# Half of a conditioning matrix-vector product taken off TensorE and given to GpSimd, in a two-block transformer kernel

## The reference, cut to what matters

```python
mod = jax.nn.silu(c) @ ada_w[l] + ada_b[l]            # [1, 1024] @ [1024, 6144]
sh_m, sc_m, g_m, sh_f, sc_f, g_f = jnp.split(mod, 6, axis=-1)
hn = adaln(x, mix_norm_g[l], sh_m, sc_m)              # rmsnorm(x) * g * (1 + scale) + shift
...                                                   # projections, four attentions, w_out
x = x + g_m[:, None, :] * y
hn = adaln(x, ffn_norm_g[l], sh_f, sc_f)
...                                                   # SwiGLU (layer 0) or 8 experts (layer 1)
x = x + g_f[:, None, :] * f
```

## Time and profile before

| | |
|---|---|
| median of 3 runs | 2811.58 us (2811.15 to 2815.84) |
| the profiled execution | 2816.96 us, of which the span of its instructions is 2815.1 us |
| TensorE busy | 2707.3 us, 96% of the span |
| VectorE busy | 1712.9 us, 61% |
| ScalarE busy | 1319.6 us, 47% |
| GpSimd busy | 27.1 us, 1% |
| HBM read | 625.06 MB, 222 GB/s over the span |
| granted TensorE clock | 0.984 of 2.4 GHz over the span |

### The profile page before, as it was taken

The page is one execution under the profiler, slowest core; times in us unless marked ns, Lnnn a source line. Parts: engine busy times, 40 slices in busy tenths (PEclk is TensorE's granted clock), DMA queues, the critical chain, the costliest instruction groups (busy, mean ns, idle before and its releaser), DMA issues.

```text
span 2815.1 us, 39528 instructions
## 1 busy us (share of the span) xinstructions
PE 2707.3 (96%) x14014; PEld 2252.2 (80%) x14014; DVE 1712.9 (61%) x2565; ACT 1319.6 (47%) x1923; POOL 27.1 (1%) x40
## 2 busy tenths in 40 slices
PE   8998999998999999998999999899999999999998
PEld 7686998885769988886998876787877878787876
DVE  1212775452117753453553453798898989898897
ACT  2212444411125432232341232677777777777776
POOL 0100000000000000000000000000000000000000
PEclk9999999999999999999999999999999999999999
DMA  7243443321434444434554334598998989898997
GB/s 310 102 150 135 185 195 147 105 90 50 160 141 168 194 178 159 148 137 165 212 191 144 135 135 142 216 372 336 344 355 321 380 323 373 332 368 335 343 348 291
DMA packets 87635, 627.32 MB, mean 223 GB/s; under 512 B 9760, under 2 KB 9920, under 8 KB 12800
## 3 DMA queue, kind: packets, MB, share of 16 engines
q1 hardware_dynamic: 84512, 613.45, 58.1%
q0 software_dynamic: 2480, 11.31, 1.1%
q10 hardware_dynamic: 560, 1.38, 0.1%
HBM read 625.06 MB, written 1.05 MB: 222 GB/s over the span
## 4 chain that ended last, share of the span: by engine, by line
PE 94%; DVE 3%; ACT 1%; issue 1%; DMA 0%; DVEq 0%; SPq 0%; ACTq 0%
PE bank L836 22%; PE bank L729 14%; PE bank L551 11%; PE bank L864 11%; PE bank L743 7%; PE bank L683 6%; PE bank L562 6%; PE bank L925 6%; PE bank L630 2%; PE bank L594 2%; PE bank L971 1%; PE bank L879 1%; PE bank L806 1%; PE bank L616 1%; PE bank L851 1%
## 5 line engine op out<-in xcount | busy, mean ns | idle before, releaser
L1324 ACT ACTIVATE sb_parts<-sb_ring 128x1024 fp32r<-128x1024 f32 x873 | 873.0, 1052 | 95.3 <-PE bank L743 47.3
L1964 DVE TENSOR_TENSOR sb_parts<-sb_ring,sb_parts 128x1024 fp32r<-128x1024 f32 x675 | 786.6, 1217 | 6.6 <-ACT sb_parts L1324 6.6
L836 PE MATMUL bank<-sb_parts 128*128 128x512 f32 x2688 | 662.0, 396 | 8.1 <-DVE sb_parts L1964 5.6
L836 PEld LDWEIGHTS bank<-sb_parts 128*128 128x128 f32 x2688 | 495.6, 188 | 118.1 <-issue 9.4
L729 PE MATMUL bank<-sb_parts 128*128 128x256 f32 x3168 | 391.3, 286 | 20.1 <-DVE sb_parts L1928 20.1
L729 PEld LDWEIGHTS bank<-sb_parts 128*128 128x128 f32 x3168 | 390.1, 195 | 22.9 <-issue 20.8
L864 PE MATMUL bank<-sb_parts 128*128 128x512 f32 x1344 | 323.9, 390 | 0.0
L864 PEld LDWEIGHTS bank<-sb_parts 128*128 128x128 f32 x1344 | 251.7, 188 | 52.1
L551 PE MATMUL bank<-sb_XT,sb_ring 128*128 128x256 f32 x1152 | 258.9, 386 | 7.0 <-DVE sb_XT L1786 4.0
L551 PEld LDWEIGHTS bank<-sb_XT,sb_ring 128*128 128x128 f32 x1152 | 221.8, 194 | 41.5 <-issue 11.0
L1928 DVE TENSOR_TENSOR sb_parts<-sb_ring,sb_parts 128x1024 fp32r<-128x1024 f32 x198 | 232.5, 1219 | 33.6 <-ACT sb_parts L1324 33.4
(11 more groups left out here) (330 smaller groups left out, 2198.4 us busy)
## 6 DMA issues: line engine op xcount, KB each, us to landing
sb_ring<-in_moe_panels SPq DMA_DIRECT2D x342, 1024.0 KB, 5.5
sb_ring<-in_ada_w SPq DMA_DIRECT2D x48, 1024.0 KB, 4.8
sb_ring<-in_ffn_w_up SPq DMA_DIRECT2D x44, 1024.0 KB, 4.9
sb_ring<-in_ffn_w SPq DMA_DIRECT2D x33, 1024.0 KB, 5.0
sb_ring<-in_w_in SPq DMA_DIRECT2D x26, 1024.0 KB, 4.8
sb_ring<-in_ffn_w_down SPq DMA_DIRECT2D x22, 1024.0 KB, 7.0
sb_ring<-in_xattn_wkv SPq DMA_DIRECT2D x16, 1024.0 KB, 4.8
sb_ring<-in_od_w_in SPq DMA_DIRECT2D x12, 1024.0 KB, 4.7
```

The lines of the kernel that those rows point to most:

```text
L836: m = nc.tensor.matmul(banks[par][:, :], x[:, k, :], w[:, cols], start=k == 0 and t == 0, stop=k == KD - 1 and t == 2, skip_group_check=True)
L1324: return nc.scalar.activation(out, in_, ACT.Copy)
L1964: V_.tensor_tensor(LOW[u], ring[slot][:, 1024 * c:1024 * c + 1024], HIGH[u], ALU.subtract) \
```

## The change

The 26 panels leave the attentions of block two. Each is loaded into the ring just ahead of a named projection panel ("lent", `LENT_AHEAD`), 5 in xat0, 8 in mix1, 4 in xat1, 5 in mix2, 4 in mix3. GpSimd multiplies it by the conditioning vector in place and sums its eight blocks into one (four instructions, each waited for) in one of three tiles `LENTS`; that releases the ring slot. Before it reuses a tile, GpSimd waits for TensorE's `take` of the panel three before. `take` sums over the 128 partitions: for a gate one matmul with 256 columns, for a shift or scale two matmuls with one column, which give the column form at once. VectorE's `taken` adds the bias with one instruction. The other 22 panels are multiplied as before. By the order of the panels 10 of the 26 are gates. That order does not change, so each is now worked off earlier.

```diff
+        LENTS = sb("LENTS", 3, T)
...
         ADA_AT = {"xat0": 2, "ffn0": 2, "mix1": 2, "xat1": 2, "ffn1": 2, "mix2": 4,
-                  "s0": tuple(s for s in range(20) if s % 4), "ffn2": 3, "mix3": 3,
-                  "s1": tuple(range(0, 20, 2)) + (19,), "ffn3": 2}
+                  "ffn2": 3, "mix3": 3, "ffn3": 2}
+        LENT_AHEAD = {"xat0": (("xq", 0, 0), ("xq", 0, 2), ("xk", 0, 0), ("xv", 0, 0), ("xv", 0, 2)),
+                      "mix1": (("qkv", 0), ("qkv", 2), ("qkv", 4), ("u", 0), ("u", 1), ("vz", 0), ("vz", 1), ("gate", 0)),
+                      "xat1": (("xq", 1, 0), ("xq", 1, 2), ("xv", 1, 0), ("xv", 1, 2)),
+                      "mix2": tuple(("s0", x) for x in ("b_qd", "a_q", "a_v", "c_k", "d_q")),
+                      "mix3": tuple(("s1", x) for x in ("b_qd", "a_q", "a_v", "c_k"))}
...
+            def lend(stage):
+                lent.append((state["panel"], ADA_ORDER[ada_done[0]], stage))
+                ada_panels[state["panel"]] = ADA_ORDER[ada_done[0]]
+                ada_done[0] += 1
+                released[state["panel"]] = (sem("panel_summed"), len(lent))
+                state["panel"] += 1
+
+            def take(hook, n, bank=None):
+                first = sum(len(x) for x in taken_by.values())
+                taken_by[hook] = list(range(first, first + n))
+                ps = claim_aside(("taken", hook)) if bank is None else claim(("taken", hook), bank)
+                for x, i in enumerate(taken_by[hook]):
+                    pe.wait_ge(sem("panel_summed"), i + 1)
+                    if lent[i][1][2] in (2, 5):
+                        m = nc.tensor.matmul(ps[:, x * T:x * T + T], cst("ones"), LENTS[:, i % 3, :], start=True, stop=True)
+                    else:
+                        for c in range(2):
+                            m = nc.tensor.matmul(ps[:, x * T + c:x * T + c + 1], LENTS[:, i % 3, c * P:c * P + P],
+                                                 cst("ones")[:, 0:1], start=True, stop=True)
+                filled(m, ("taken", hook))
...
+            def sum_lent(stage):
+                for i, (n, _, of) in enumerate(lent):
+                    if of != stage:
+                        continue
+                    pool.wait_ge(landed[n % RING], 16 * (n // RING + 1))
+                    if i >= 3:
+                        hook = [h for h, x in taken_by.items() if i - 3 in x][0]
+                        wait_full(pool, ("taken", hook))
+                    w = ring[n % RING][:, :].rearrange("p (k n) -> p k n", k=KD)
+                    step(G.tensor_tensor(w, w, sm("cond", 8).rearrange("p (k o) -> p k o", o=1).broadcast_to([P, KD, T]),
+                                         ALU.mult))
+                    step(G.tensor_tensor(w[:, 0:4, :], w[:, 0:4, :], w[:, 4:8, :], ALU.add))
+                    step(G.tensor_tensor(w[:, 0:2, :], w[:, 0:2, :], w[:, 2:4, :], ALU.add))
+                    m = G.tensor_tensor(LENTS[:, i % 3, :], w[:, 0, :], w[:, 1, :], ALU.add)
+                    m.then_inc(sem("panel_summed"), 1)
```

More of the change, by code:

```diff
@@ L638, in attention @@
                             m.then_inc(sem("unit_mixed"), 1)
+                    if key[0] == "x" and s == 5:
+                        take((f"xat{key[1]}", 1), 2, 7)
+                        if key[1] == "0":
+                            take((f"xat{key[1]}", 2), 1, 6)
                     if key[0] == "s" and s == DIFF_SUMS:
@@ L999, in _ @@
                 panel_T(("qkv", j))
+                if j == 3:
+                    take(("mix1", 0), 1)
             ps = claim_aside("l2")
@@ L1011, in _ @@
             panel_T(("qkv", 5))
+            take(("mix1", 1), 1)
             pe.wait_ge(sem("norms_spread"), 2)
@@ L1030, in _ @@
             panel_T(("u", 1))
+            take(("mix1", 2), 1)
             wait_read(("bb", 0), ("bb", 1))
@@ L1036, in _ @@
             panel_tok(("vz", 0))
+            take(("mix1", 3), 1)
             for tb in range(NT):
@@ L1046, in _ @@
                     panel_T(("xk", 1, lv - 4), rhs=MT)
+                if lv > 1:
+                    take(("mix1", lv + 2), 1)
                 pe.wait_ge(sem("level_ready"), lv)
@@ L1168, in _ @@
                 panel_T((k2, "c_q"))
+                take((n, 0), 2, 6)
                 for j in range(2, 4):
@@ L1188, in _ @@
                 panel_tok((k2, "d_v"))
+                take((n, 1), 2, 7)
+                if layer == 0:
+                    take((n, 2), 1, 5)
                 pe.wait_ge(sem("rope_done"), layer + 1)
@@ L1879, in cross @@
                     evac(("xk", layer, j), KT[:, 2 * j:2 * j + 2, :])
+                taken((n, 0))
                 attention(f"x{layer}")
+                taken((n, 1))
+                if layer == 0:
+                    taken((n, 2))
                 add_sum(n)
@@ L2169, in _ @@
             convolve(3)
+            taken(("mix1", 0))
             convolve(4)
@@ L2175, in _ @@
             convolve(5)
+            taken(("mix1", 1))
             for name, t, scale in (("rq", gQ, P ** -0.5), ("rk", gK, 1.0)):
@@ L2198, in _ @@
                 read_out(m, ("kt", tb))
+            taken(("mix1", 2))
             for name, dst, decay in (("a", gA, gD), ("at", gAT, gDT)):
@@ L2212, in _ @@
                                           flat(gDT)[:, 512 * tb:512 * tb + 512], ALU.mult), ("qk", tb))
+            taken(("mix1", 3))
             wait_drained(dve, ("qk", 0), ("qk", 1))
@@ L2255, in _ @@
                         step(V_.tensor_tensor(u_, tmp, u_, ALU.mult))
+                if lv > 1:
+                    taken(("mix1", lv + 2))
                 evac((("y", lv), 1), flat(gY)[:, 512:1024], bank_of((("y", lv), 1))[:, :])
@@ L2409, in _ @@
                 m.then_inc(sem("band_bias_ready"), 1)
+                for x in range(2 if layer else 3):
+                    taken((n, x))
                 attention(k2, layer)
```

40 lines of the change are left out of this document (35 added, 5 removed).

## The result

The changed kernel takes 2790.11 us, median of nine runs (2788.57 to 2804.92). The kernel before, on the same basis, takes 2815.84 us (2811.15 to 2819.66). The ratio is 0.9918, 95% interval 0.9901 to 0.9935: 0.8% faster, some 23 us by the ratio and 25.7 by the medians. The forecast was 2768 us, 1.6%; the time lies in the range, but nearly half of the expected gain is missing. The profiled execution of after has a span of 2786.7 us, 28.4 less than before's 2815.1.

What follows compares the result with a forecast made beforehand. TensorE, busy 96% of the span, was taken as the bound. -92.6 + 17.4 + 12.3 + 9.3 + 6.5 + 4 = -43.1 us, against the median of 2811.58 gives 2768 us, 1.6% faster; range 2744 to 2795.

Steps and rivals of the forecast that it cites:

- Removed, 92.6 us: TensorE in the attentions of mix2 and mix3: 26 panels at 3.56 us each leave its queue, 92.6 us.
- What is left of a step: Attention steps without a panel take 2.66 us, TensorE barely still the bound; three places break that and cost 17.4 us together.
- the start: Start of both attentions: TensorE waits for VectorE's mask addition, taken instructions and scalings, 5.1 us in mix2, 4.5 in mix3, 9.6 together.
- the square root: ScalarE, once in each attention: two table loads of 1.28 us and about 0.2 of work, costing 2.1 us each, 4.2 together.
- the selection biases: VectorE in the attentions: 1.22 us each against 0.5 free, 2.8 us for four, plus 0.8 for the normalisation, 3.6.
- Takes, 12.3 us: Work added on TensorE: 16 shifts or scales at 0.49 us, 7.9, and ten gates at 0.44 us, 4.4; sum 12.3.
- GpSimd in time, no late panel: GpSimd's sums, 195 to 234 us in all, are ready before each take, and no panel lands late in the ring: cost 0.
- What GpSimd disturbs, 9.3 + 6.5 us: GpSimd's instructions hold up VectorE's: 9.3 us at the norms of xat0, mix1, mix2 and mix3, 6.5 within mix1.
- level 1: In mix1, five mask products on VectorE meet two panels on GpSimd, so level 1 comes about 3 us late.
- The clock, 4 us: TensorE behind some eight new waits of 2.4 us: a third lose 1.7 us each to the clock, 4 us; bounds 0 and 14.
- The rival of the clock: Panel-free attention steps fall to 1.2 GHz, 2.66 us more in 40 steps, 106 us: 2874 us; two slower cases 0.09 together.
- the rival with more contention: Mix1's two-operand VectorE instructions all wait for GpSimd, steps lose their slack: 2784 to 2800 us, chance 0.2.

Runs made afterwards that it cites:

- the kernel with the late panels: Kernel before, nothing lent, with the attentions' 26 panels moved to steps 5 to 19 of mix2 and 9 to 19 of mix3: 2846.10 us, ratio 1.0104.
- the run without sums: Changed kernel with three of GpSimd's four instructions per panel left out, which sends tokens to other experts: 3786.46 us, 1.3446; read only up to ffn3's transposes.

## Why the prediction was off

- **Removed, 92.6 us.** Right: 26 panels are gone from TensorE's queue. L973 has 352 records (22 panels x 16), and a panel is worth 3.50 us in the kernel with the late panels. TensorE's busy time in the attentions, less what the clock cost, fell by 91.7 us.
- **What is left of a step.** Right: 2.66 us, TensorE still the bound. Without the clock the attentions would have given 58.7 + 20.4 = 79.1 us, more than the forecast 75.2. TensorE's idle time in them grew by 12.6 us, where 17.4 were forecast; the start was sized well (waits of 4.20 and 0.78 us in mix2, 3.61 and 0.78 in mix3: 9.4 us, forecast 9.6), the square root and the selection biases were taken some 5 us too dear.
- **Takes, 12.3 us.** 9.7 by the run without sums.
- **GpSimd in time, no late panel.** Right; 215.4 us of sums.
- **What GpSimd disturbs, 9.3 + 6.5 us.** The places were right. The waits are 2.61 us in xat0 (forecast 2), 3.03 in mix1 (2.8), 4.68 in mix2 (2.8), 1.85 in mix3 (1.7) and 2.39 at level 1 (about 3). In mix2 both scalings were held up, not the second alone. In all, GpSimd's work cost 14.8 us of waits, where these terms make 15.8, and some 3 us of clock.
- **The clock, 4 us: this step failed.** It said that eight new waits of 2.4 us might each cost 1.7 us, a third of them. Measured: 33 us more are not granted over the span. Where TensorE was at work it is 23 us more, 20.4 of them in the attentions, beyond the upper bound of 14. The granted clock over the attentions was 0.78 and 0.88, and below 0.9 was a sign that the prediction had named for being wrong. The error was the unit. A row of one group behind a wait shows what that group loses; it does not show how long the lower level lasts. In attentions without panels at the start it lasted two to eight steps. And the cause named, a wait, was wrong as well: with the wait of 4.20 us cut to 0.80 the level fell all the same, and in the run with the wait as it was, eight filler matmuls brought it back before the next scores.
- **The rival of the clock** had the mechanism and nearly the price (2.66 us a step; measured 2.29), and asked for 16 steps of 40 to undo the gain. It came for 10 of 40, some of them in part. I gave it as all or nothing and left its middle out, for want of a row: mix0's steps, which ran at 1.00, are two, and stand behind dense work.
- That the range held the time is luck: it reached so far up because of the rival with more contention, right in time (2784 to 2800) and wrong in its mechanism, since the waits came out as forecast or smaller, and what was missing was clock.
- The forecast was set against the median of three runs, 2811.58 us. Against the later 2815.84 the same sum gives 2772.7.

In sum, against the forecast's -43.1: attentions 16.5 us short (clock 20.4 and work removed 0.9, less 4.8 on the waits), GpSimd 4.6 over (clock 3.0, the start 1.8, the rest small), takes 2.6 under, the rest 0.2, and the 4 us set aside for the clock to be taken off: 14.7 us, and -43.1 + 14.7 = -28.4, the measured difference of the spans.

What stays open: why the level falls at the start of an attention and rises some 10 to 40 us later with the same steps, what decides whether dense matmuls there hold it, and what brought on the low clock in mix1's 8.2 us. The kernel that would have parted the takes from GpSimd's part in one step, all 26 panels multiplied on TensorE at the places of the takes, deadlocks in that order and has no time.

## What to carry to other kernels

Work taken off a busy TensorE can also take away what held its clock up: where it leaves a stretch of small matmuls that wait for one another, look at the granted clock of that stretch first, and price a fall by how long the level stays, not by the first group behind a wait. A few panels left at the start of such a stretch can be nearly free (4 panels of 14.2 us cost nothing, 8 of 28.5 us cost 6.5 us in one kernel and 14.5 in another), and even matmuls that nobody reads, in a wait that is there anyway, paid for themselves. Starting GpSimd's work behind VectorE's instructions that TensorE waits for took 12 us of waits and slow rows away, but not reliably time: 5 and 3 us less in two kernels, 8 more in a third, where the clock fell elsewhere.

## What had not been expected of the hardware

- The lower level lasts while TensorE is busy: granted clock 0.50 for 23.62, 28.52 and 33.55 us with TensorE busy 97 or 98% of each, then 1.00 with no change of work.
- In one place the level came back under sixteen dense records of 128 rows and 256 columns (5.34 us for 3.56 us of work); with the wait removed instead it did not. But behind two whole panels, one in step 0 and one in step 1 of mix3's attention, it fell in one trace and stayed at 0.50 for 17.13 us, TensorE busy for all of it, while another trace of the same matmuls shows 0.98 over that attention.
- The same instructions of mix1 took 205.35 and 214.05 us in two kernels, so a few us of difference in one stage of one trace prove nothing by themselves.
- The first 128 projection records, before any changed instruction, took 27.86 us in the trace of before, 29.79 in that of after and 27.86 again in the kernel without sums, so about 2 us of a comparison can be decided in the first 45 us. That is clock too, though the profile reads 1.00 there: its first record of the granted clock, at 1.00, comes at 13.68, 19.73 and 14.59 us, and counts as full speed what lies ahead of it. If TensorE ran at half speed until then, the projection, which starts at 15.83 us in after, would lose (19.73 - 15.83) / 2 = 1.95 us; measured are 1.93. The same estimate comes out within 0.02 us in all fourteen traces.
- Two VectorE scalings with one SBUF operand took 7.72 us beside GpSimd's copy, multiplication and addition, and 2.07 where it started behind them.
